# x loaded and turned by columns, projected before it is normalised, and the stick-breaking mask added in PSUM by VectorE

## The chip, the cores and the metric

One core of one Trainium2 chip. The metric is the device time of one execution in microseconds (us); lower is better. The number compared is the median over runs. Clock of TensorE: 2.4 GHz at its upper level, 1.2 GHz at its lower one.

## The reference

One block of a streaming encoder, with a sequence of 512 tokens and width 2048, all in float32:

```python
u = rms_norm(x, norm_gain)                      # x / sqrt(mean(x^2) + eps) * gain, per token
proj = u @ w_in                                 # 2048 -> 13392 columns
# split: q,k,v,z of 8 "sb" heads; q,k,v,z of 8 "sa" heads; q_ix (16 x 64), k_ix (64), w_ix (16); 2 gates
# sb head: z = q.k / sqrt(128), strictly causal (s < t)
#   w[t,s] = exp(log_sigmoid(z) + sum over s<j<t of log_sigmoid(-z[t,j])), 0 where s >= t;  o = w @ v
# indexer: score[t,s] = sum over h of w_ix[t,h] * relu(q_ix[t,h] . k_ix[s]);  top 128 keys of each query
# sa head: softmax over the chosen keys with ALiBi;  o = p @ v
mixed = sigmoid(g_sb) * (o_sb * silu(z_sb)) @ w_branch_sb + sigmoid(g_sa) * (o_sa * silu(z_sa)) @ w_branch_sa
out = rms_norm(x + mixed @ w_out, final_norm_gain)
```

The top-k choice of a query does not change when its scores are all multiplied by one positive number, and relu passes a positive factor through. The gain belongs to a feature, the root-mean-square factor (`rstd` below) to a token.

## The kernel before

**Products.** Each float32 product is made of three TensorE products of rounded parts: a value is copied by ScalarE into a rounded "hi" part, VectorE subtracts to get the "lo" part, and `mm3` adds hi x hi, lo x hi and hi x lo in PSUM. A product has 128 x 128 weights and 512 columns.

**Chunks and strips.** All projections stream their weights. A chunk `c` is 512 output columns (34 chunks in all); it is made of 8 strips `s`, each of two k-tiles of 128 rows (512 KB), loaded by SyncE into one of two buffers `stage`. ScalarE makes `w_hi` (`split_hi`), VectorE `w_lo` (`split_lo`), both two strips ahead (`LEAD`) in a ring of four, and TensorE runs the 24 products of a strip into the four banks `proj`. Each engine has one instruction stream in program order; between the strips other work stands as a list of steps (`chunk(c, steps)`). Semaphores tie the streams: SyncE loads a strip only when `strip_lo` says that the buffer's last user is split.

**The start.** Chunks 0 and 1 make the indexer's queries. `u` must be there transposed (features on partitions): `u_hi`, `u_lo`, 16 k-tiles of 512 tokens. x comes as four row tiles `xs[:, i, :]` of 1 MB. For each, ScalarE sums squares (`sum_of_squares`), VectorE makes `rstd` (`row_scale`, six small steps and a root on ScalarE) and scales the first 512 columns in place (`normal`); TensorE turns them with the identity (`turn_x`), and the copy out of PSUM multiplies by the gain (`turned_u_high`, `turned_u_low`). Only when the fourth row tile is done has tile 0 of `u` all its tokens. Between these transposes TensorE multiplies zeros (`keep_busy`, tile `blank`). The remaining columns are normalised in one go (`normal(i, slice(CW, D_MODEL))`) and turned between the strips of chunk 0, where the 80 columns of the index keys and weights are projected too (`index_keys`, bank `kw_bank`).

**The sb heads.** While chunks 10 to 17 stream, one sb head is worked off beside each. Step 0: scores z into the four banks `attn` (block i holds keys 128i.. against the queries from 128i on). Step 1 to 3: ScalarE takes abs, exp and ln (`e_tile`), VectorE completes softplus(z) and multiplies the 128 x 128 diagonal block by the 0/1 mask `before` (`softplus`). Step 4: TensorE adds to z the negated sums of softplus over later keys (weights `neg_tri`, `neg_one`), and last, with `big_ident` (1e30 times the identity), one 128-column product that puts -1e30 where the key is not before the query. Step 5: ScalarE takes exp.

The order of all of this is written by hand; nothing plans it. The functions that the change touches, with the profile's line numbers:

Of the kernel before, what the change touches and what calls it, by code (L numbers as in the profile page):

```python
# [25 lines left out]
D_MODEL, SEQ = 2048, 512  # L26
# [4 lines left out]
P = 128  # L31
# [30 lines left out]
def build(nc, x, norm_gain, w_in, w_branch_sb, w_branch_sa, w_out, final_gain, out):  # L62
# [57 lines left out]
    blank = at("blank", [CW], R, place["late"] + 4 * P)  # L120

# [24 lines left out]
    big_ident = at("big_ident", [P], R, place["const"] + 4 * P)  # L146
# [31 lines left out]
    def unit(kp, late):  # L178
        return 2 * kp + late

    UNITS = KT
    FIRST_TURNED = {0: 1, 2: 2, 1: 3, 3: 4}
    UNIT_BANK = [attn[j] for j in (0, 1, 3, 2)] + [attn[(j - 4) % 3] for j in range(4, UNITS)]
    BEFORE_IT = {4: 0, 5: 1, 6: 3}
# [7 lines left out]
    x_rows = x[0].rearrange("(i p) d -> i p d", p=P)  # L192
# [10 lines left out]
    x_loaded = [sem(f"x_loaded{i}") for i in range(QT)]  # L203
    gain_loaded, ixw_loaded, consts, masks = sem("gain_loaded"), sem("ixw_loaded"), sem("consts"), sem("masks")
    sumsq, norm_step, rooted, xn_ready = sem("sumsq"), sem("norm_step"), sem("rooted"), sem("xn_ready")
    gain_turned, gain_ready, blank_ready = sem("gain_turned"), sem("gain_ready"), sem("blank_ready")
    xt_done, u_hi_ready, u_lo_ready = sem("xt_done"), sem("u_hi_ready"), sem("u_lo_ready")
    ixw_hi_ready, ixw_lo_ready, kw_done, kw_copied = sem("ixw_hi_ready"), sem("ixw_lo_ready"), sem("kw_done"), sem("kw_copied")
    kix_hi_ready, kix_lo_ready = sem("kix_hi_ready"), sem("kix_lo_ready")
    wix_turned, wix_ready, dist_ready, far_ready = sem("wix_turned"), sem("wix_ready"), sem("dist_ready"), sem("far_ready")  # L210
# [5 lines left out]
    z_done, e_step, e_ready, sp_step, sp_ready = sem("z_done"), sem("e_step"), sem("e_ready"), sem("sp_step"), sem("sp_ready")  # L216
# [46 lines left out]
    with block:  # L263

        @block.sync
        def _(sp):
            for i in range(QT):
                sp.dma_start(xs[:, i, :], x_rows[i]).then_inc(x_loaded[i], 16)
                if i == 0:
                    sp.dma_start(gain_rows[0:KT, :], norm_gain[0].rearrange("(t p) -> t p", p=P)  # L270
                                 ).then_inc(gain_loaded, 16)

            def load_strip(c, s, src):

                if not (isinstance(c, int) and NS * c + s < 2):
                    sp.wait_ge(strip_lo, c * NS + (s - 1))
                sp.dma_start(stage[:, s % 2, :, :], src).then_inc(strip_loaded[s % 2], 16)
                if isinstance(c, int) and NS * c + s == 1:
                    sp.dma_start(ixw[:, :, :], win[:, :, COL_KIX:COL_KIX + KW]).then_inc(ixw_loaded, 16)
# [12 lines left out]
            for c in range(C_QIX, C_SB):  # L292
                load_chunk(c, rows(win), COL_QIX + CW * c)
# [18 lines left out]
        def _(pool):  # L312
# [14 lines left out]
            pool.wait_ge(xn_ready, 2 * QT)  # L327
# [38 lines left out]
        def _(act):  # L366
# [33 lines left out]
            def turned_u_high(n):  # L400

                act.wait_ge(xt_done, FIRST_TURNED[n] if n < 4 else n + 1)
                tokens = slice(2 * P * (n % 2), 2 * P * (n % 2) + 2 * P)
                for j in range(2):
                    k = 2 * (n // 2) + j
                    A(u_hi[:, k, tokens], UNIT_BANK[n][:, 2 * P * j:2 * P * j + 2 * P], ACT.Copy,
                      scale=gain[:, k:k + 1]).then_inc(u_hi_ready, 1)

            def sum_of_squares(i):
                act.wait_ge(x_loaded[i], 16)  # L410
                if i:
                    act.wait_ge(sumsq, i)
                A(junk[:, :], xs[:, i, :], ACT.Square, accum_out=ss[:, i:i + 1]).then_inc(sumsq, 1)

            def root_of(i):
                act.wait_ge(norm_step, 6 * i + 1)
                A(root[:, i:i + 1], var[:, i:i + 1], ACT.Sqrt).then_inc(rooted, 1)

            nc.scalar.preload_act_table_set("sqrt_and_others")
            sum_of_squares(0)  # L420
            root_of(0)
# [974 lines left out]
```

## Time and profile before

| | us |
|---|---|
| median of 3 runs | 1637.13 (1636.83 to 1637.85) |
| the profiled execution | 1636.94 |
| its span, first to last instruction | 1635.3 |
| TensorE busy | 1622.2 (99%) |
| VectorE, ScalarE, GpSimd busy | 768.0 (47%), 588.1 (36%), 16.1 (1%) |
| mean granted TensorE clock | 0.999 |
| moved by DMA | 165.90 MB, 101 GB/s over the span |

Busy time counts an instruction from its start to its end. Matmuls overlap (one of 512 columns takes about 390 ns, the next starts 227 ns after it), so their pace is read from starts, not from the busy time.

### The profile page before, as it was taken

How to read it: one execution, taken by the hardware profiler on the slowest of the kernel's cores; microseconds unless marked ns; L12 is line 12 of the kernel's file. 1: busy time of each engine (PE TensorE's matmuls, PEld its weight loads, DVE VectorE, ACT ScalarE, POOL GpSimd, SP SyncE). 2: the span in 40 equal slices, each digit the busy share in tenths (PEclk: the TensorE clock that was granted, in tenths of full speed). 3: DMA queues.
4: the chain of work that ended last, by engine and by line, in shares of the span. 5: the costliest groups of instructions: out<-in, count | busy, mean ns of one | idle time of the engine just before them, and what ended most of it. 6: DMA issues, size and time to landing. Idle time of an engine off the chain costs nothing.

```text
span 1635.3 us, 20353 instructions
## 1 busy us (share of the span) xinstructions
PE 1622.2 (99%) x7402; PEld 1351.3 (83%) x7402; DVE 768.0 (47%) x1151; ACT 588.1 (36%) x942; POOL 16.1 (1%) x37
## 2 busy tenths in 40 slices
PE   8999999999999999999999999999999999999998
PEld 6888888888888888888888888888888888888886
DVE  5334578622125444455544455445455554444333
ACT  5333333222225454445443233333323533322222
POOL 0000000000000000000000000000000000000000
PEclk9999999999999999999999999999999999999999
DMA  5232323332333323232333232332233422253233
GB/s 203 71 103 78 88 80 90 103 94 86 103 103 91 96 83 88 78 103 83 97 87 115 89 102 84 96 96 85 82 103 95 175 97 96 97 198 125 90 107 116
DMA packets 82043, 165.90 MB, mean 101 GB/s; under 512 B 7104, under 2 KB 7632, under 8 KB 80848
## 3 DMA queue, kind: packets, MB, share of 16 engines
q1 hardware_dynamic: 77808, 150.10, 30.3%
q0 software_dynamic: 3040, 13.63, 2.2%
q10 hardware_dynamic: 1152, 1.57, 0.3%
q8 instruction: 29, 0.48, 0.1%
q14 instruction: 14, 0.11, 0.0%
HBM read 156.90 MB, written 8.39 MB: 101 GB/s over the span
## 4 chain that ended last, share of the span: by engine, by line
PE 99%; DVE 1%; DMA 0%; ACT 0%; issue 0%; SPq 0%; DVEq 0%
PE proj L1130 28%; PE proj L1132 28%; PE proj L1131 28%; PE attn L1131 3%; PE attn L1132 3%; PE attn L1130 3%; PE proj L1198 1%; PE attn L1290 1%; PE attn L1324 1%; PE attn L1252 1%; PE attn L1251 1%; PE attn L1178 0%; PE attn L1295 0%; DMA gain_rows<-in_norm_gain 0%; DVE xs L751 0%; PE attn L1297 0%
## 5 line engine op out<-in xcount | busy, mean ns | idle before, releaser
L1130 PE MATMUL proj<-u_hi,w_hi 128*128 128x512 f32 x1536 | 599.9, 391 | 0.1
L1131 PE MATMUL proj<-u_lo,w_hi 128*128 128x512 f32 x1536 | 598.1, 389 | 0.0
L1132 PE MATMUL proj<-u_hi,w_lo 128*128 128x512 f32 x1536 | 598.0, 389 | 0.0
L696 DVE TENSOR_TENSOR w_lo<-stage,w_hi 128x1024 fp32r<-128x1024 f32 x267 | 325.9, 1223 | 512.5 <-ACT w_hi L374 510.4
L374 ACT ACTIVATE w_hi<-stage 128x1024 fp32r<-128x1024 f32 x267 | 282.2, 1060 | 479.2 <-PE proj L1132 351.4
L1132 PEld LDWEIGHTS proj<-u_hi,w_lo 128*128 128x128 f32 x1536 | 288.4, 188 | 60.2
L1130 PEld LDWEIGHTS proj<-u_hi,w_hi 128*128 128x128 f32 x1536 | 288.5, 188 | 59.5 <-issue 0.5
L1131 PEld LDWEIGHTS proj<-u_lo,w_hi 128*128 128x128 f32 x1536 | 288.5, 188 | 58.7
L390 ACT ACTIVATE area<-proj 128x512 f32 (+1 forms) x80 | 47.8, 597 | 171.4 <-PE proj L1132 171.3
L1130 PE MATMUL proj<-w_hi,u_hi 128*128 128x512 f32 x256 | 99.8, 390 | 0.0
L1131 PE MATMUL proj<-w_lo,u_hi 128*128 128x512 f32 x256 | 99.6, 389 | 0.0
L1132 PE MATMUL proj<-w_hi,u_lo 128*128 128x512 f32 x256 | 99.6, 389 | 0.0
L1130 PE MATMUL proj<-w_hi,area_r 128*128 128x512 f32 x216 | 84.0, 389 | 0.0
L1131 PE MATMUL proj<-w_lo,area_r 128*128 128x512 f32 x216 | 84.0, 389 | 0.0
L1132 PE MATMUL proj<-w_hi,area_r 128*128 128x512 f32 x216 | 84.0, 389 | 0.0
L1132 PEld LDWEIGHTS proj<-w_hi,u_lo 128*128 128x128 f32 x256 | 48.1, 188 | 10.0
L1131 PEld LDWEIGHTS proj<-w_lo,u_hi 128*128 128x128 f32 x256 | 48.1, 188 | 9.9
L1130 PEld LDWEIGHTS proj<-w_hi,u_hi 128*128 128x128 f32 x256 | 48.1, 188 | 9.8
L877 DVE RECIPROCAL og<-og 128x512 f32<-128x512 f32 x16 | 53.7, 3354 | 0.5
L471 ACT ACTIVATE relu<-attn 128x256 f32<-128x256 f32 (+2 forms) x48 | 21.0, 490 | 89.9 <-PE attn L1252 89.9
L818 DVE SCALAR_TENSOR_TENSOR score<-relu,wix,score 128x256 f32<-128x256 f32 (+2 forms) x45 | 27.8, 619 | 47.0 <-ACT relu L471 44.2
L1130 PE MATMUL attn<-u_hi,w_hi 128*128 128x512 f32 x128 | 49.8, 389 | 0.0
(184 smaller groups left out, 1444.9 us busy)
## 6 DMA issues: line engine op xcount, KB each, us to landing
stage<-in_w_in SPq DMA_DIRECT2D x208, 512.0 KB, 3.7
stage<-in_w_out SPq DMA_DIRECT2D x32, 512.0 KB, 3.6
stage<-in_w_branch_sb SPq DMA_DIRECT2D x16, 512.0 KB, 3.6
stage<-in_w_branch_sa SPq DMA_DIRECT2D x16, 512.0 KB, 3.9
xs<-in_x SPq DMA_DIRECT2D x4, 1024.0 KB, 8.1
o_scratch<-og POOLq DMA_DIRECT2D x16, 256.0 KB, 2.3
hres<-in_x POOLq DMA_DIRECT2D x1, 4096.0 KB, 13.6
o_in<-o_scratch POOLq DMA_DIRECT2D x3, 1024.0 KB, 5.9
```

The costliest lines, as they stand in the source:

```text
L374: A(w_hi[:, s % RING, :, :], stage[:, s % 2, :, :], ACT.Copy).then_inc(strip_hi, 1)
L390: A(dst(e), proj[e][:, :], ACT.Copy).then_inc(proj_free, 1)
L471: A(relu[:, n % 2, 0:WQ[qi]], attn[h % 4][:, 0:WQ[qi]], ACT.Relu).then_inc(relu_ready, 1)
L696: V.tensor_tensor(w_lo[:, s % RING, :, :], stage[:, s % 2, :, :], w_hi[:, s % RING, :, :].bitcast(F), ALU.subtract).then_inc(strip_lo, 1)
L818: V.scalar_tensor_tensor(acc, relu[:, n % 2, 0:w], wix[:, qi, h:h + 1], acc, ALU.mult, ALU.add).then_inc(relu_used, 1)
L877: V.reciprocal(og[:, :], og[:, :]).then_inc(silu_step, 1)
L1130: nc.tensor.matmul(out_, a_hi, b_hi, start=start, stop=False, skip_group_check=free)
L1131: nc.tensor.matmul(out_, a_hi, b_lo, start=False, stop=False, skip_group_check=free)
L1132: return nc.tensor.matmul(out_, a_lo, b_hi, start=False, stop=stop, skip_group_check=free)
L1198: nc.tensor.matmul(proj[3][:, :], blank[:, 0:P], blank[:, :], start=True, stop=True)
L1251: nc.tensor.matmul(o_, q, kix_lo[:, 0:WQ[qi]], start=True, stop=False)
L1252: nc.tensor.matmul(o_, q, kix_hi[:, 0:WQ[qi]], start=False, stop=True).then_inc(dots_done, 1)
```

## The change

**x.** SyncE loads x as eight column pairs, `x_loaded[p]`: all 512 tokens of 256 features, 512 KB in runs of 1 KB. They are interleaved with the first strips of weights. The gain's load moves to ScalarE's queue. TensorE turns tile k as soon as its pair is there (four 128 x 128 transposes of raw x), 0 and 1 before the first product, 2 and 3 in the middle of strip 0, the others two strips ahead. Strip 0 runs its four banks for the first k-tile and then for the second, so that it can start with half of its weights split.

**u.** Chunk 0 is projected from x times gain, without the token's factor. Tiles from 4 on, and a second time 0 to 3, are copied to SBUF as "raw" tiles (`turned_raw`), times gain; `u_hi` and `u_lo` are made from these. The sums of squares are taken in halves, beside the strips. `rstd` is brought into a row over the tokens by four more transposes (`rstd_cols`, `rstd_row`), the raw tiles are multiplied by it (`scale_raw`), and `u_hi`, `u_lo` are overwritten with the normalised values from the end of chunk 0 through chunk 1 (`normal_high`, `normal_low`). The index keys are projected after strips 5, 6 and 7 from the raw tiles and scaled by the row; the index weights of the first eight index heads get `rstd` once more, since those heads' queries come from chunk 0.

**The mask.** VectorE makes `hide` (0 where the key is before the query, -1e30 elsewhere) and adds it to the diagonal block of each z in PSUM (`mask_z`) before ScalarE reads z. The multiplication by `before` in `softplus` and the products with `big_ident` are gone; ScalarE's `e_tile` waits for `z_masked` instead of `z_done`.

```diff
-            for i in range(QT):
-                sp.dma_start(xs[:, i, :], x_rows[i]).then_inc(x_loaded[i], 16)
...
+            load_x(0)
+            first_strip(0)
+            load_x(1)
+            first_strip(1)
+            for p in range(2, 5):
+                load_x(p)
+            first_strip(2)
+            for p in range(5, NS):
+                load_x(p)
+            first_strip(3)
+            sp.dma_start(ixw[:, :, :], win[:, :, COL_KIX:COL_KIX + KW]).then_inc(ixw_loaded, 16)
...
@@ ScalarE: the start, and the steps between the strips of chunk 0
+            turned_high(0)
+            act.wait_ge(strip_loaded[0], 16)
+            A(w_hi[:, 0, 0, :], stage[:, 0, 0, :], ACT.Copy).then_inc(first_hi, 1)
+            turned_high(1)
+            A(w_hi[:, 0, 1, :], stage[:, 0, 1, :], ACT.Copy).then_inc(strip_hi, 1)
             split_hi(0, 1)
+            turned_high(2)
+            turned_high(3)
+            for i in range(QT):
+                sum_of_squares(i, 0)
+
+            def in_first(s):
                 def f():
+                    if s + 2 < NS:
+                        turned_pair(s + 2)
+                    if s in (1, 2):
+                        for i in (2 * s - 2, 2 * s - 1):
+                            sum_of_squares(i, 1)
...
+                    elif s == NS - 1:
+                        normal_high(0)
+                        normal_high(1)
...
@@ VectorE: a raw tile, and the steps between the strips of chunk 0
+            def turned_raw(k):
+                dve.wait_ge(xt_done, k + 1)
...
+                V.tensor_scalar(raw_u(k), by_tile(turn_bank(k)[:, :]), gain[:, k:k + 1], None,
+                                ALU.mult).then_inc(raw_ready, 1)
...
+            def in_first(s):
                 def f():
+                    if s + 2 < NS:
+                        for k in (2 * s + 4, 2 * s + 5):
+                            turned_raw(k)
+                        for k in (2 * s + 4, 2 * s + 5):
+                            turned_low(k)
+                    if s == 3:
+                        dve.wait_ge(sumsq, 2 * QT)
...
+                        rsqrt(slice(0, QT), 1, 1)
...
+                            V.tensor_scalar(rstd_cols[:, i, :], neg_one[:, :].bitcast(F), rstd[:, i:i + 1], -1.0,
+                                            ALU.mult, ALU.mult).then_inc(cols_ready, 1)
...
+                    elif s == 4:
+                        dve.wait_ge(cols_turned, 1)
+                        V.tensor_copy(rstd_row[:, :], kw_bank[:, :]).then_inc(row_ready, 1)
...
+                    elif s in (5, 6):
+                        scale_raw(2 * s - 10)
+                        scale_raw(2 * s - 9)
...
@@ VectorE: an sb head
+                def mask_z(o):
+                    t = attn[QT - 1 - o][:, 0:P]
+                    dve.wait_ge(z_done, n * 4 + o + 1)
+                    V.tensor_tensor(t, t, hide[:, :], ALU.add).then_inc(z_masked, 1)
+
...
-                                           ALU.max, ALU.add).then_inc(sp_step, 1)
-                    dve.wait_ge(sp_step, n * 4 + o + 1)
-                    t = full[:, o % 2, 0:P]
-                    V.tensor_tensor(t, t, before[:, :], ALU.mult).then_inc(sp_ready, 1)
+                                           ALU.max, ALU.add).then_inc(sp_ready, 1)
...
                 def s1():
+                    for o in range(QT):
+                        mask_z(o)
                     v_low(n, n + 2 * HEADS)
                     softplus(0)
...
@@ TensorE: the start
-            keep_busy(14)
...
+            keep_busy(1)
+            turn_x(0)
+            turn_x(1)
+            keep_busy(4)
...
@@ TensorE: step 4 of an sb head
-                        nc.tensor.matmul(attn[i][:, 0:P], big_ident[:, :], neg_tri[:, :], start=False, stop=True,
-                                         skip_group_check=True).then_inc(c_done, 1)
+                        m.then_inc(c_done, 1)
```

**How instructions move.** TensorE, from the program's start to the first products of strip 0, before (`blank` is the tile of zeros, `attn` the banks that receive transposes, `proj` those of a chunk):

```order
L1198 MATMUL proj<-blank 128x512 x4
L1204 MATMUL attn<-ident,gain_rows 128x16
L1198 MATMUL proj<-blank 128x512 x14
L1178 MATMUL attn<-ident,xs 128x128 x4
L1198 MATMUL proj<-blank 128x512 x9
L1178 MATMUL attn<-ident,xs 128x128 x4
L1198 MATMUL proj<-blank 128x512 x11
L1178 MATMUL attn<-ident,xs 128x128 x4
L1198 MATMUL proj<-blank 128x512 x8
L1178 MATMUL attn<-ident,xs 128x128 x4
L1198 MATMUL proj<-blank 128x512 x7
L1130 MATMUL proj<-u_hi,w_hi 128x512
```

And the same place of the changed kernel:

```order
L1303 MATMUL proj<-blank 128x512 [waits blank_ready]
L1303 MATMUL proj<-blank 128x512 x3
L1309 MATMUL attn<-ident,gain_rows 128x16 [waits gain_loaded,masks]
L1303 MATMUL proj<-blank 128x512
L1290 MATMUL attn<-ident,xs 128x128 [waits x_loaded0]
L1290 MATMUL attn<-ident,xs 128x128 x7
L1303 MATMUL proj<-blank 128x512 x4
L1241 MATMUL proj<-u_hi,w_hi 128x512 [waits first_lo,u_lo_ready]
```

Ahead of the first product stand eight transposes instead of sixteen and nine products of zeros instead of 53, and the first of them waits for one pair of columns instead of all rows.

ScalarE of the changed kernel, from its first copy of a turned tile to the split of strip 3 (`junk,ssq` is a half sum of squares; before, the sums stood ahead of everything, as four of 2048 elements):

```order
L435 ACTIVATE u_hi<-attn,gain 128x512 [waits xt_done,gain_ready]
L468 ACTIVATE w_hi<-stage 128x512 [waits strip_loaded0]
L435 ACTIVATE u_hi<-attn,gain 128x512 [waits xt_done]
L470 ACTIVATE w_hi<-stage 128x512
L405 ACTIVATE w_hi<-stage 128x1024 [waits strip_loaded1]
L435 ACTIVATE u_hi<-attn,gain 128x512 [waits xt_done] x2
L458 ACTIVATE junk,ssq<-xs 128x1024 [waits x_loaded2,x_loaded3,x_loaded1,x_loaded0]
L458 ACTIVATE junk,ssq<-xs 128x1024 [waits sumsq] x3
L405 ACTIVATE w_hi<-stage 128x1024 [waits strip_loaded0]
L438 ACTIVATE u_hi<-area 128x512 [waits raw_ready] x2
L405 ACTIVATE w_hi<-stage 128x1024 [waits strip_loaded1]
```

The four half sums now stand ahead of the split of strip 2, on which VectorE's part of strip 2 and the load of strip 4 hang.

TensorE, step 4 of an sb head (the two last blocks, `attn2` and `attn3`), before:

```order
L1290 MATMUL attn2<-x_lo_66,neg_tri_98 128x256
L1290 MATMUL attn2<-x_hi_64,neg_tri_98 128x256
L1295 MATMUL attn2<-x_lo_66,neg_one_99 128x128
L1295 MATMUL attn2<-x_hi_64,neg_one_99 128x128
L1297 MATMUL attn2<-neg_tri_98,big_ident_97 128x128
L1290 MATMUL attn3<-x_lo_66,neg_tri_98 128x128
L1290 MATMUL attn3<-x_hi_64,neg_tri_98 128x128
L1297 MATMUL attn3<-neg_tri_98,big_ident_97 128x128
```

And of the changed kernel:

```order
L1414 MATMUL attn2<-x_lo_66,neg_tri_100 128x256
L1414 MATMUL attn2<-x_hi_64,neg_tri_100 128x256
L1419 MATMUL attn2<-x_lo_66,neg_one_101 128x128
L1419 MATMUL attn2<-x_hi_64,neg_one_101 128x128
L1414 MATMUL attn3<-x_lo_66,neg_tri_100 128x128
L1414 MATMUL attn3<-x_hi_64,neg_tri_100 128x128
```

One product of 128 columns is gone from each of the four blocks, and nothing stands in its place.

## Rows read from the trace of the kernel before

**Rows 1.** The page, busy times (part 1) and the last chain (part 4).

```profile
PE 1622.2 (99%) x7402; PEld 1351.3 (83%) x7402; DVE 768.0 (47%) x1151; ACT 588.1 (36%) x942; POOL 16.1 (1%) x37
PE 99%; DVE 1%; DMA 0%; ACT 0%; issue 0%; SPq 0%; DVEq 0%
```

**Rows 2.** Waits of TensorE: us in total, times, longest.

```profile
PE attn L1204 <- DMA gain_rows<-in_norm_gain: 2.6, 1, 2.6
PE proj L1198 <- DVE blank L728: 1.7, 1, 1.7
PE attn L1178 <- DVE xs L751: 0.8, 1, 0.8
```

**Rows 3.** Timeline of TensorE, the start: start us, us.

```profile
6.47 4.82 PE L1198 MATMUL proj<-blank 128*128 128x512 f32 x14
...
21.22 0.47 PE L1130 MATMUL proj<-u_hi,w_hi 128*128 128x512 f32 x1
...
26.56 0.39 PE L1132 MATMUL proj<-u_hi,w_lo 128*128 128x512 f32 x1
27.71 1.09 PE L1178 MATMUL attn<-ident,xs 128*128 128x128 f32 x8 [0.76 <-DVE xs L751]
```

**Rows 4.** Timeline of TensorE: between two strips, and where chunk 2 starts.

```profile
34.13 1.04 PE L1178 MATMUL attn<-ident,xs 128*128 128x128 f32 x8
34.93 0.47 PE L1130 MATMUL attn<-u_hi,ixw_hi 128*80 128x512 f32 x1
...
126.35 0.39 PE L1130 MATMUL proj<-u_hi,w_hi 128*128 128x512 f32 x1
```

**Rows 5.** Tiles xs and stage up to 60 us, in that order.

```profile
DMA to landing us min/median/max: 5.0/8.1/11.1
...
DMA to landing us min/median/max: 3.5/3.7/12.6
```

**Rows 6.** Windows: busy time of each engine, clock, DMA share, GB/s.

```profile
8.00:12.00 4.00, 4.00 (x18) 3.27 (x17) 2.08 (x11) 3.07 (x6) 0.00 (x0) 1.00 1.00 422
12.00:15.00 3.00, 3.00 (x16) 2.46 (x15) 1.91 (x10) 2.56 (x6) 0.00 (x0) 1.00 1.01 391
15.00:18.00 3.00, 3.00 (x17) 2.47 (x16) 1.90 (x8) 2.78 (x4) 0.00 (x0) 1.00 1.07 281
```

**Rows 7.** Groups of 0 to 131 us, by shape: busy us, mean ns.

```profile
L696 DVE TENSOR_TENSOR w_lo<-stage,w_hi 128x1024 fp32r<-128x1024 f32 x19 | 23.1, 1220 | 22.7 <-ACT w_hi L374 22.5
L374 ACT ACTIVATE w_hi<-stage 128x1024 fp32r<-128x1024 f32 x19 | 20.0, 1065 | 21.5 <-PE proj L1132 15.8 <-DMA stage<-in_w_in 5.6
L801 DVE TENSOR_TENSOR area_r<-proj,area_r 64x512 fp32r<-64x512 f32 x16 | 11.0, 689 | 12.4 <-ACT area_r L461 12.1
L461 ACT ACTIVATE area_r<-proj 64x512 fp32r<-64x512 f32 x16 | 9.5, 592 | 13.4 <-PE proj L1132 12.9
L413 ACT ACTIVATE junk<-xs 128x2048 f32<-128x2048 f32 x4 | 7.7, 1914 | 4.3 <-DMA xs<-in_x 3.8 <-ACT gain L423 0.5
L751 DVE TENSOR_SCALAR xs<-xs,rstd 128x512 f32<-128x512 f32 x4 | 1.9, 486 | 0.1
```

**Rows 8.** Timeline of TensorE, step 4 of the second sb head.

```profile
571.57 0.22 PE L1297 MATMUL attn<-neg_tri,big_ident 128*128 128x128 f32 x1
571.63 0.39 PE L1290 MATMUL attn<-x_lo,neg_tri 128*128 128x384 f32 x1
...
572.79 0.27 PE L1297 MATMUL attn<-neg_tri,big_ident 128*128 128x128 f32 x1
572.90 0.27 PE L1290 MATMUL attn<-x_lo,neg_tri 128*128 128x128 f32 x1
```

**Rows 9.** Timelines of TensorE and VectorE, the same head.

```profile
570.77 0.39 PE L1290 MATMUL attn<-x_lo,neg_tri 128*128 128x512 f32 x1
...
548.56 0.29 DVE L893 SCALAR_TENSOR_TENSOR full<-attn,eb 128x128 f32<-128x128 f32 x1 [0.85 <-ACT eb L517]
...
559.72 0.69 DVE L903 TENSOR_TENSOR x_lo<-full,x_hi 128x512 fp32r<-128x512 f32 x1 [0.23 <-ACT x_hi L522]
```

More of the change, by code:

```diff
@@ L120, in build @@
     blank = at("blank", [CW], R, place["late"] + 4 * P)
+    rstd_row = at("rstd_row", [SEQ], F, place["late"] + 4 * P + 4 * CW)
+    rstd_cols = at("rstd_cols", [QT, P], F, work + 14 * TILE)
     SUM_W = (WK[2], WK[1])
@@ L174, in build, with turn_bank, bank_user, keys_slot @@
     kw_bank = attn[3]
[L178 to L184, printed above, removed]
+    TURN_BANKS = 3
+    HEAD_START = 4
+    ROW_SLOT = 4
+    KEY_SLOTS = {5: (0, 1, 2), 6: (3, 4, 5), 7: (6, 7)}
+    def turn_bank(k):
+        return attn[k] if k < HEAD_START else attn[(k - HEAD_START) % TURN_BANKS]
+    def bank_user(k):
+        return k - HEAD_START if k < HEAD_START + TURN_BANKS else k - TURN_BANKS
+    def keys_slot(p):
+        return [slot for slot, pairs in KEY_SLOTS.items() if p in pairs][0]
+    def raw_u(k):
+        return by_tile(area[:, 24 + k, :]) if k < KT // 2 else xs[:, :, P * k - D_MODEL // 2:P * k - D_MODEL // 2 + P]
+    def by_tile(ap):
+        return ap.rearrange("p (i t) -> p i t", i=QT)
     o_dram = nc.dram_tensor("o_scratch", (2 * HEADS, P, SEQ), F, kind="Internal").ap()
@@ new lines, in scale_raw, with normal_low @@
+            def scale_raw(p):
+                for k in (2 * p, 2 * p + 1):
+                    dve.wait_ge(raw_ready, k + 1)
+                    V.tensor_tensor(raw_u(k), raw_u(k), by_tile(rstd_row[:, :]), ALU.mult).then_inc(raw_scaled, 1)
+            def normal_low(p):
+                for k in (2 * p, 2 * p + 1):
+                    dve.wait_ge(un_hi_ready, k + 1)
+                    V.tensor_tensor(by_tile(u_lo[:, k, :]), raw_u(k), by_tile(u_hi[:, k, :].bitcast(F)),
+                                    ALU.subtract).then_inc(un_lo_ready, 1)
@@ new lines, in _, with first_strip @@
+            turn_x(0)
+            turn_x(1)
+            keep_busy(4)
+            def first_strip():
+                for j in range(2):
+                    pe.wait_ge(u_lo_ready, j + 1)
+                    if j == 0:
+                        pe.wait_ge(first_lo, 1)
+                    else:
+                        turn_x(2)
+                        turn_x(3)
+                        pe.wait_ge(strip_lo, 1)
+                    for e in range(4):
+                        cols = slice(P * e, P * e + P)
+                        m = mm3(proj[e][:, :], w_hi[:, 0, j, cols], w_lo[:, 0, j, cols],
+                                u_hi[:, j, :], u_lo[:, j, :], j == 0, False)
+                m.then_inc(strip_used, 1)
@@ L1232, in turn_wix @@
                 m.then_inc(wix_turned, 1)
[L1234 to L1236 removed]
+            chunk(C_QIX + 1, [None] * 6 + [turn_wix], ready=lambda t: pe.wait_ge(un_lo_ready, t + 1))
             def dots(qi, s):
```

300 lines of the change are left out of this document (161 added, 139 removed).

## The prediction

> **What bounds the kernel now.** I read the page first: TensorE is busy 99% of the span, and the chain that ended last is TensorE's own for 99% [rows 1]. So time goes down only where TensorE has fewer products in its stream, or where its useful stream starts earlier. The list of waits then shows how little waiting there is: three waits, 5.1 us together, all of them before 28 us [rows 2]. What the list does not show is that TensorE is "busy" with zeros at the start. In the timeline the first real product of a strip starts at 21.22; before it stand 53 products of zeros and 16 transposes, while x is loaded, summed and scaled [rows 3]. The reader should see that 21.2 us of 1635.3 are a prologue, and that after strip 0 (last product issued at 26.56, its slot over at 26.79) another 0.92 us pass until the transposes at 27.71, which wait for VectorE's scaling of the remaining columns. Behind that TensorE never waits again, so what shortens the prologue should reach the end whole, if the other engines keep up. Chunk 2 starts at 126.35 [rows 4], where both kernels have the same work left; I work out that point for the changed kernel.
>
> **The start, step by step.** A transfer of 512 KB that goes alone lands 3.5 us after its issue; the first 1 MB of x, with others queued behind it, took 5.0 [rows 5]. The difference is 1.5 us for half a megabyte, 350 GB/s. The first pair of columns is such a 512 KB transfer, issued first: at about 0.94, as x is now, so it lands at 4.4. Its runs are 1 KB, which no row shows. The bounds are the 2 KB runs of weights (391 GB/s) and the stretch with the 320-byte rows of the index weights (281 GB/s) [rows 6]; I take 350 for it, nearer to the first, since 1 KB is nearer to 2 KB. Strip 0 is next in the queue, 1.3 us more, and the gain has its own queue and is small, so neither is late: strip 0 by 5.9, gain by 3.6 to 4.5.
> Then a chain: four transposes to 4.8 (0.1 us each, 0.80 for eight [rows 4]; up to twice that at the low clock, so 5.2 with the way to ScalarE), u_hi of tile 0 as ScalarE's 512 elements out of PSUM (592 ns) to 5.8, half of w_hi (half of 1065 ns) to 6.4, half of w_lo (half of 1220 ns, 0.65 with its start) to 7.2, and the way to TensorE [rows 7]. The changed stream has its zeros in the same time: five products and eight transposes. The first product starts at about 7.5 instead of 21.22: 13.7 earlier.
>
> **What TensorE does from there to chunk 2.** Now it takes 126.35 - 21.22 = 105.13 us. Strips and index keys are the same 432 products. Changes:
> - minus 0.92, the wait after strip 0, whose cause (scaling in one go, rows 2) is gone;
> - plus 8 transposes of x that used to stand ahead of 21.22, plus 4 of the factor: 12 x 0.1 = 1.2;
> - the clock. The burst of fourteen products of zeros from 6.47 takes 4.82 us, where at 227 ns each it would need about 3.35 [rows 3]: some 7 or 8 of the fourteen ran at half pace, 0.42 apart, after the wait for the gain (2.6 us, rows 2). The granted clock reads 1.00 in the window from 8 on all the same [rows 6], so I go by the spacing. Ahead of the first product the changed stream has five products of zeros and eight transposes behind the gain, less than that; I let 3 products of strip 0 still be slow, 0.19 each, 0.6 in all. If it were a dozen, 2.3.
> - a wait before strip 2. ScalarE has twelve instructions ahead of its split of strip 2: after the copies of tiles 2 and 3, which end at 12.6, four half sums at half of 1914 ns plus reading the sum, 1.15 each, to 17.2; then w_hi at 1065 ns to 18.3, VectorE's w_lo to 19.5, two raw tiles, then u_lo of tiles 4 and 5. A raw tile is a multiplication by a column out of PSUM. VectorE's 512 elements take 486 ns by tensor_scalar from SBUF and 689 when it reads PSUM in tensor_tensor [rows 7]; these are the bounds, and I take 0.69, the row that reads PSUM. This gives 22.2 for u_lo of tile 5, against 21.5 at which TensorE wants it (7.5 + 11.0 for 48 products + 1.6 + 0.8 of transposes + 0.6): 0.7 late.
> - a wait in front of the four transposes of the factor after strip 4. VectorE has 1.15 + 4 x 0.69 = 3.9 us of work for each strip, against a pace of 5.5 + 0.8 = 6.3. In strip 3's slot it gets some 4.2 more (the factor in seven small steps, four copies of 128 elements, ixw_lo of 1280 elements at the pace of w_lo, 1.5): 8.1, so it falls 1.8 behind, having been 1 to 1.5 ahead: 0.7.
> Together 105.13 - 0.92 + 1.2 + 0.6 + 0.7 + 0.7 = 107.4, so chunk 2 starts at 114.9, 11.45 earlier.
>
> One page bears on the price of the raw tile. The Trainium skill (VectorE: DVE Perf Modes, Why PSUM operands drop a tier) says that a float32 operand in PSUM holds VectorE at its plain rate, the doubled rate of a tensor_scalar being one for SBUF. By that rule 0.69 stands; without it, at 0.49, both waits would shrink to 0.4 together and chunk 2 start 1.0 earlier. No row here shows a tensor_scalar of 512 elements out of PSUM.
>
> The rest of the new work costs nothing as long as its cover lasts. VectorE's fullest slot behind the factor is strip 5's: 1.15 and eight instructions of 0.69 (two raw tiles, two u_lo, four scalings), 6.7 us, against 5.5 + 0.8 + 4.1 (eighteen products of index keys) = 10.4 on TensorE. In chunk 1 it has 1.15 + 4 x 0.69 = 3.9 and ScalarE 1.07 + 2 x 0.6 = 2.3 a strip, under 5.5. The first normalised tiles are written after strip 6 is used; TensorE has then index keys, strip 7 and index keys again, 4.1 + 5.5 + 2.7 = 12.3 us, against 4 x 0.6 + 4 x 0.69 = 5.2 for both pairs. Loads: x and four strips are 6.3 MB, at 350 GB/s 18 us behind 2.0: x's last pair is there about 18, wanted after strip 5, beyond 40. Without that cover each microsecond late would be one of the total.
>
> **The mask.** Behind a 384-column product the product with big_ident takes 0.06 us (571.57 to 571.63), among 128-column ones 0.11 (572.79 to 572.90) [rows 8]. Two of each in a head: 0.34, eight heads: 2.7. For it VectorE gets four additions of 128 elements in PSUM and loses as many multiplications by the 0/1 mask in each head. Reading 128 elements out of PSUM takes softplus's first block 0.29 us [rows 9], which I take for an addition. It stands earlier though: all four wait for z, and v_low and the first softplus are queued behind them, 1.7 us later than now; ScalarE's first e_tile comes 0.3 later and its next split of weights with it. The cover: the last x_lo ends at 560.41 and TensorE asks for it at 570.77, 10.4 us later [rows 9], and weights are split two strips, over 10 us, ahead. Cost 0; a saving of 2.7 on the path, since TensorE has no wait there. The lower bound is 0, if something else fills the slots.
>
> **Sum.** -11.45 - 2.7 = -14.2. The profiled execution took 1636.94 (span 1635.3), which becomes 1622.8; it lies 0.2 under the median of 1637.13, so I predict 1622.9.
>
> **The rivals.**
> - *Forecast*: 1621 to 1625, chance 0.70.
> - *The front goes better*: the raw tile at 0.49, columns at the weights' 391 GB/s, full pace from the first product. Then -13.4 - 2.7: 1621.0, and 1620 if the first pair lands half a microsecond sooner. For it: no row proves any wait. Against: strip 0 must be halved by two engines anyway. 0.08, outside the forecast.
> - *The columns come slowly.* At 200 GB/s, below the worst window, the first product starts at 8.5, and tiles 4 to 9 are late by 0.4 to 1.9 us each, 8 in all; chunk 2 only 4.5 earlier: 1630. Against it: runs of 2 KB do 391. 0.06.
> - *The clock stays low through strip 0.* All 24 products at half pace lose 24 x 0.2 = 4.8 instead of 0.6, but 0.7 of the first late wait is swallowed: 1626.4. For it: the stream has a gap for the gain and one for x, and behind the 2.6 us for the gain the pace was low now too [rows 2, 3]. 0.10.
> - *The mask saves nothing*: 1625.6. Only if TensorE waited there. 0.02.
> - *Slower*: the masks hold up VectorE's queue in each sb head. The place is x_lo and sum_lo before step 4. It costs nothing until the chain through e_tile, softplus and splits is 10.4 us later than now, and eight times the excess from there. To end over 1640.4 it must be 12.6 us late; I find 1.7. 0.02.
> The remaining 0.02 is for two of the small ones together.
>
> **Chances.** A measurement of this kernel tells a change from none at about 0.2%, 3.3 us. Faster by over that (below 1633.9): 0.96; within it 0.02; slower 0.02. The range takes in the forecast, most of the better front and the low clock: 1619.8 to 1627.0.
>
> **What would show it.** The first product of strip 0 in the timeline at 7 to 8 us; waits of TensorE for u_lo before strip 2 and for the factor's copies, both under 1.5 us; none in chunk 1; chunk 2's first product at 114 to 116; raw tiles at 0.69; step 4 of a head 0.34 shorter, with no wait of TensorE for x_lo, sum_lo or z_masked. The prediction is wrong if x's first pair lands after 6, if the waits for u_lo repeat strip by strip, or if products beyond the first ten run 0.42 apart.

## The result, and the profile after

| | before | after |
|---|---|---|
| median, us | 1637.49 (1636.83 to 1637.94, 4 runs) | 1622.35 (1622.05 to 1623.18, 4 runs) |
| the profiled execution | 1636.94 | 1623.18 |
| its span | 1635.3 | 1621.6 |

The ratio is 0.9909, with a 95% interval of 0.9891 to 0.9926: 15.1 us less. The forecast was 1622.9, with a range of 1619.8 to 1627.0. The profiled execution of the changed kernel is the longest of its four; the spans of the other three are 1620.5 to 1620.9. The last section comes back to that 1 us.

The page of the changed kernel, parts 1 and 4, beside [rows 1]:

```profile
PE 1610.9 (99%) x7330; PEld 1340.7 (83%) x7330; DVE 789.1 (49%) x1169; ACT 594.4 (37%) x947; POOL 16.2 (1%) x37
...
PE 97%; ACT 1%; DVE 1%; DMA 0%; issue 0%; SPq 0%; ACTq 0%; DVEq 0%
```

TensorE is still the bound. Its waits, beside [rows 2] (us in total, times, longest):

```profile
PE proj L1303 <- DVE blank L780: 1.7, 1, 1.7
PE proj L1241 <- DVE u_lo L803: 0.5, 1, 0.5
PE attn L1309 <- DMA gain_rows<-in_norm_gain: 0.2, 1, 0.2
PE proj L1241 <- DVE w_lo L820: 0.2, 1, 0.2
```

The wait for the gain fell from 2.6 to 0.2 us and the one for VectorE's scaling is gone. The new ones are two short ones, for `w_lo` and for `u_lo`. TensorE's timeline shows where they stand, beside [rows 3] and [rows 4] (start us, us):

```profile
4.88 1.97 PE L1290 MATMUL attn<-ident,xs 128*128 128x128 f32 x8
6.49 2.06 PE L1303 MATMUL proj<-blank 128*128 128x512 f32 x4
8.71 0.77 PE L1241 MATMUL proj<-u_hi,w_hi 128*128 128x512 f32 x1 [0.16 <-DVE w_lo L820]
9.27 0.63 PE L1242 MATMUL proj<-u_lo,w_hi 128*128 128x512 f32 x1
9.70 0.63 PE L1243 MATMUL proj<-u_hi,w_lo 128*128 128x512 f32 x1
10.13 0.58 PE L1241 MATMUL proj<-u_hi,w_hi 128*128 128x512 f32 x1
10.54 0.39 PE L1242 MATMUL proj<-u_lo,w_hi 128*128 128x512 f32 x1
...
22.37 1.03 PE L1290 MATMUL attn<-ident,xs 128*128 128x128 f32 x8
23.94 0.47 PE L1241 MATMUL proj<-u_hi,w_hi 128*128 128x512 f32 x1 [0.53 <-DVE u_lo L803]
...
42.19 1.04 PE L1290 MATMUL attn<-ident,xs 128*128 128x128 f32 x8
43.30 0.66 PE L1338 MATMUL attn<-ident,rstd_cols 128*128 128x128 f32 x4
...
121.37 0.28 PE L1375 MATMUL attn<-kix_lo,area_r 128*128 128x256 f32 x1
```

The first product starts at 8.71 instead of 21.22. The first four hold 0.41 to 0.56 us each (half pace is about 0.43), those from 10.54 on start 0.23 apart. The slots of the eight transposes at 22.37 are over after 0.79 us, at 23.16, and strip 2 starts at 23.94: 0.78 late. The factor's transposes start 1.11 after those at 42.19: 0.32 late. The last row is the first product of a dot (`dots`), the mark that I use for the two kernels' common ground: before it stood at 131.79, so the front gives 10.4 us. The last residual of the output stands 13.8 us earlier than before. The other 3.4 us come in the eight sb heads, whose spacing is 49.48 us where it was 49.90.

Step 4 of the second sb head, TensorE's timeline, beside [rows 8]:

```profile
560.73 0.34 PE L1414 MATMUL attn<-x_lo,neg_tri 128*128 128x384 f32 x1
560.91 0.35 PE L1414 MATMUL attn<-x_hi,neg_tri 128*128 128x384 f32 x1
...
561.33 0.28 PE L1414 MATMUL attn<-x_lo,neg_tri 128*128 128x256 f32 x1
561.45 0.28 PE L1414 MATMUL attn<-x_hi,neg_tri 128*128 128x256 f32 x1
```

The same places in the kernel before, whose rows after those of [rows 8] are needed here:

```profile
571.86 0.34 PE L1290 MATMUL attn<-x_hi,neg_tri 128*128 128x384 f32 x1
...
572.33 0.33 PE L1290 MATMUL attn<-x_lo,neg_tri 128*128 128x256 f32 x1
572.50 0.28 PE L1290 MATMUL attn<-x_hi,neg_tri 128*128 128x256 f32 x1
```

The whole step took 2.47 us before (570.77 to 573.24) and takes 2.03 now (559.93 to 561.96). Of the 0.44, 0.34 are the four slots that the prediction counted. The other 0.10 stand behind two of them: before, the 384-column product that followed the short one held its slot for 0.23 us (571.63 to 571.86), where it now holds 0.18; the 256-column one 0.17 (572.33 to 572.50) instead of 0.12.

VectorE's and ScalarE's rows at the start, as their timelines give them:

```profile
6.09 0.69 ACT L435 ACTIVATE u_hi<-attn,gain 128x512 fp32r<-128x512 f32 x1 [1.69 <-PE attn L1290]
7.20 0.63 ACT L468 ACTIVATE w_hi<-stage 128x512 fp32r<-128x512 f32 x1 [0.43 <-DMA stage<-in_w_in]
...
18.78 1.04 ACT L405 ACTIVATE w_hi<-stage 128x1024 fp32r<-128x1024 f32 x1
21.78 1.29 ACT L438 ACTIVATE u_hi<-area 128x512 fp32r<-128x512 f32 x2 [1.95 <-DVE area L793]
...
19.86 1.23 DVE L748 TENSOR_TENSOR w_lo<-stage,w_hi 128x1024 fp32r<-128x1024 f32 x1 [3.38 <-ACT w_hi L405]
21.00 1.40 DVE L793 TENSOR_SCALAR area<-attn,gain 128x512 f32<-128x512 f32 x2
22.45 1.35 DVE L803 TENSOR_TENSOR u_lo<-area,u_hi 128x512 fp32r<-128x512 f32 x2
```

The chain before strip 2 reads as follows: behind four half sums ScalarE's split of strip 2 starts at 18.78, VectorE has stood still for 3.38 us and splits from 19.86, makes two raw tiles from 21.00, and u_lo of tiles 4 and 5 ends at 23.80. TensorE could have had it at 23.16. Both sides of this wait move with TensorE's first product: ScalarE's copies of tiles 2 and 3, at 13.03, have waited 2.03 us for the transposes in the middle of strip 0 (12.39), and the sums stand behind them.

### The profile page after: what moved, and what is told of

The parts are those of the page before. It is cut to its first block, busy times and chain, and to the rows that moved or that the text cites. A ratio compares the mean times of both kernels' runs of the same rounds, so it can differ in the third digit from the quotient of the medians.

```text
span 1621.6 us, 20273 instructions
## 1 busy us (share of the span) xinstructions
PE 1610.9 (99%) x7330; PEld 1340.7 (83%) x7330; DVE 789.1 (49%) x1169; ACT 594.4 (37%) x947; POOL 16.2 (1%) x37
## 4 chain that ended last, share of the span: by engine, by line
PE 97%; ACT 1%; DVE 1%; DMA 0%; issue 0%; SPq 0%; ACTq 0%; DVEq 0%
PE proj L1241 28%; PE proj L1242 28%; PE proj L1243 28%; PE attn L1242 3%; PE attn L1243 3%; PE attn L1241 3%; PE attn L1414 1%; PE attn L1447 1%; PE attn L1376 1%; PE attn L1375 1%; ACT junk L458 0%; PE attn L1419 0%; DMA stage<-in_w_in 0%; ACT w_hi L405 0%; DVE w_lo L748 0%
## 5 line engine op out<-in xcount | busy, mean ns | idle before, releaser
L990 DVE TENSOR_TENSOR og<-attn,og 128x512 f32<-128x512 f32 x16 | 11.1, 692 | 81.0 <-PE attn L1243 81.0
```

## The experiments

**One half of the change at a time.** `mask_only` is the kernel before with the mask as VectorE's addition; `front_only` is the changed kernel with the old mask. The core of the first edit (the second is its reverse in the changed kernel):

```diff
+                def mask_z(o):
+                    t = attn[QT - 1 - o][:, 0:P]
+                    dve.wait_ge(z_done, n * 4 + o + 1)
+                    V.tensor_tensor(t, t, hide[:, :], ALU.add).then_inc(z_masked, 1)
...
-                    V.tensor_tensor(t, t, before[:, :], ALU.mult).then_inc(sp_ready, 1)
...
-                        nc.tensor.matmul(attn[i][:, 0:P], big_ident[:, :], neg_tri[:, :], start=False, stop=True,
-                                         skip_group_check=True).then_inc(c_done, 1)
```

> The kernel before with the mask alone moved to VectorE. Theory (two separate parts that add up): each sb head is 0.42 us shorter, as in the changed kernel's trace (heads 49.48 apart instead of 49.90), 3.4 us in all, so 1634.1; step 4 of a head 2.03 us instead of 2.47. By my prediction's term (0.34 a head) it is 1634.8. Rival (TensorE waits for the later softplus somewhere when the start is not also changed): under 2 us, 1635.5 or more.

> The changed kernel with the old mask. Theory (separate parts): chunk 2 starts at 115.9 as in the changed kernel, 10.4 us before the old kernel, heads 49.90 apart; the time is the changed kernel's plus 3.4, 1625.7. Rival (the parts help each other): more than 0.5 us off that sum.

Measured: `mask_only` 1634.28 (1633.63 to 1634.61, 11 runs), `front_only` 1625.94 (1625.77 to 1626.33, 5 runs), the kernel before 1637.65 in the same comparison (15 runs); ratios 0.9979 (0.9970 to 0.9988) and 0.9930 (0.9917 to 0.9944). The mask alone gives 3.4 us, 0.42 a head, the front alone 11.7. Their sum, 15.1, is the whole change: neither part hides or eats the other. What a removed slot is worth is read from the traces, since the interval of `mask_only` (2.0 to 4.9 us) holds the predicted 2.7 as well. The heads of `mask_only` stand 49.48 us apart and its step 4 takes 2.02 us (570.89 to 572.91), as in the changed kernel; the heads of `front_only` stand 49.90 apart. So it is not 0.34 us a head but 0.42 to 0.44.

**Where ScalarE's sums stand.** `sums_split` moves two of the four first half sums behind the split of strip 2 and the tiles 4 and 5.

```diff
-            for i in range(QT):
+            for i in (0, 1):
                 sum_of_squares(i, 0)
...
-                    if s in (1, 2):
+                    if s == 0:
+                        for i in (2, 3):
+                            sum_of_squares(i, 0)
+                    elif s in (1, 2):
```

> The changed kernel with the half sums of squares of row tiles 2 and 3 moved behind the split of strip 2 and the copies of tiles 4 and 5 on ScalarE. Theory (the wait before strip 2 comes from ScalarE's four sums ahead of its split): the split of strip 2 comes 2.4 us earlier, the wait of 0.8 us before strip 2 is gone, no new one before strip 3, chunk 2 starts 0.8 earlier: about 1621.6. Rival (the wait comes from VectorE's raw tiles or from the load of strip 2): the wait stays over 0.5 us, 1622.4.

Measured: 1622.66 (1622.36 to 1622.81, 4 runs), ratio 0.9909 (0.9894 to 0.9924), no gain that can be told from the changed kernel, where 1621.6 was expected. The line that is new in the list of TensorE's waits says why (us in total, times, longest):

```profile
PE attn L1341 <- DVE rstd_cols L851: 0.7, 1, 0.7
```

The wait for `u_lo` before strip 2 is gone, and TensorE now waits 0.7 us for the factor's columns. In its timeline the factor's transposes start at 42.90, 1.73 behind the transposes of x at 41.17, so 0.94 late where it was 0.32. From strip 0's second group of transposes to the first dot it takes 108.85 us, against 108.98 in the changed kernel: 0.13 of the 0.78 was kept. The time had not gone, it had moved. The reason is a loop. In each strip VectorE's raw tiles wait for its `w_lo`, which waits for ScalarE's `w_hi`; and ScalarE's `u_hi` waits for the raw tiles, for 1.95 us in the row at 21.78 above. ScalarE's rows in `sums_split` give the loop's period, with its timeline of strips 3 to 5:

```profile
22.57 1.04 ACT L405 ACTIVATE w_hi<-stage 128x1024 fp32r<-128x1024 f32 x1
25.56 1.29 ACT L438 ACTIVATE u_hi<-area 128x512 fp32r<-128x512 f32 x2 [1.95 <-DVE area L796]
...
28.98 1.04 ACT L405 ACTIVATE w_hi<-stage 128x1024 fp32r<-128x1024 f32 x1
```

From split to split it takes 6.41 us, with two sums in each round behind `u_hi`. TensorE's own strip with its transposes takes 6.33 to 6.37. So nothing was caught up by the time that the factor was due. Without sums in it the same loop took 4.19 us in the changed kernel (18.78 to 22.97), so it is the sums' place in the loop that makes it as long as a strip.

**The sums in ScalarE's pause.** `gap` puts two half sums into exactly that pause, in each of the strips 0 to 3, and none ahead of strip 2's split.

```diff
-            for i in range(QT):
-                sum_of_squares(i, 0)
...
+                    if s < 4:
+                        for i in (2 * (s % 2), 2 * (s % 2) + 1):
+                            sum_of_squares(i, s // 2)
                     if s + 2 < NS:
                         turned_pair(s + 2)
-                    if s in (1, 2):
-                        for i in (2 * s - 2, 2 * s - 1):
-                            sum_of_squares(i, 1)
```

> The changed kernel with all eight half sums of squares in ScalarE's pause between the split of the next strip and the two tiles of u_hi, two for each of the strips 0 to 3, and none ahead of strip 2's split. In the profile of sums_split ScalarE stood still there for 1.95 us a strip, waiting for VectorE's raw tiles, and two sums take 2.3 us. Theory (the 0.8 us before strip 2 and the 0.3 us before the factor's transposes are both the price of where ScalarE's sums stand, and its pause can take them): both waits are gone or under 0.1 us, the stretch from the transposes after strip 0's first half to the first dots is 107.9 instead of 108.98, and the median is 1621.3 (1621.0 to 1621.8), with an allowance for the moment at which the start's pace rises. Rival 1 (the loop ScalarE, VectorE, ScalarE is as long as a strip, so any sum in it delays the tiles of strips 3 to 5): the wait before strip 2 is gone, a wait of 0.5 to 1.0 comes back before strips 4 or 5 or the factor's transposes, 1622.3 to 1622.8. Rival 2 (the sums of the second half now wait for x pairs that land late): a pause over 1 us at strip 2, over 1623.

Measured: 1621.19 (1621.11 to 1621.49, 4 runs), the kernel before 1637.43 (7 runs) beside it, ratio 0.99 (0.9884 to 0.9917). It is the fastest version of this study, level with `gap_half3` below. Waits of TensorE and its timeline:

```profile
PE attn L1307 <- DMA gain_rows<-in_norm_gain: 0.3, 1, 0.3
```

```profile
8.56 0.56 PE L1239 MATMUL proj<-u_hi,w_hi 128*128 128x512 f32 x1
8.96 0.39 PE L1240 MATMUL proj<-u_lo,w_hi 128*128 128x512 f32 x1
...
11.48 1.03 PE L1288 MATMUL attn<-ident,xs 128*128 128x128 f32 x8
...
119.39 0.28 PE L1373 MATMUL attn<-kix_lo,area_r 128*128 128x256 f32 x1
```

The other wait in its list is the 1.7 us for the zeros' tile; the list shows no wait of TensorE from its first product on, and in the timeline the factor's transposes start 0.88 us after those ahead of them, so 0.09 late. From 11.48 to 119.39 it takes 107.91 us, where the changed kernel takes 108.98 (12.39 to 121.37): 1.07 less, nearly all of the two late steps of 0.78 and 0.32. Both were the price of where the sums stood.

**Strip 0 in halves.** `half_strip` loads strip 0 as two transfers of 256 KB, so that its first half can be split before the second is there.

```diff
+                if s == 0:
+                    for j, loaded in ((0, half_loaded), (1, strip_loaded[0])):
+                        sp.dma_start(stage[:, 0, j, :], win[:, j, COL_QIX:COL_QIX + CW]).then_inc(loaded, 16)
+                    return
...
-            act.wait_ge(strip_loaded[0], 16)
+            act.wait_ge(half_loaded, 16)
             A(w_hi[:, 0, 0, :], stage[:, 0, 0, :], ACT.Copy).then_inc(first_hi, 1)
             turned_high(1)
+            act.wait_ge(strip_loaded[0], 16)
```

> The changed kernel with strip 0 loaded as two transfers of 256 KB, one for each k-tile, ScalarE waiting only for the first ahead of its first split. Theory (the first product waits for strip 0's load, which lands 0.4 us after ScalarE is free): the first split starts at 6.8 instead of 7.2 and the first product at 8.3 instead of 8.7; as products run at half pace until about 10.5 anyway, chunk 2 starts only 0.2 earlier: 1622.2. Rival (start and end move together, the pace rises that much earlier too): 0.4 to 0.5 earlier, 1621.9. Rival (two small transfers take longer than one): no gain, or up to 0.5 later.

Measured: 1622.52 (1622.22 to 1622.70, 4 runs), no difference. Timelines of ScalarE and TensorE:

```profile
6.75 0.62 ACT L472 ACTIVATE w_hi<-stage 128x512 fp32r<-128x512 f32 x1
...
8.47 0.61 PE L1246 MATMUL proj<-u_hi,w_hi 128*128 128x512 f32 x1
```

And ScalarE's row of `sums_split`, where strip 0 comes as one load:

```profile
6.77 0.62 ACT L468 ACTIVATE w_hi<-stage 128x512 fp32r<-128x512 f32 x1
```

Beside the changed kernel's profiled execution the half of `w_hi` starts 0.45 sooner and the first product 0.24 sooner. That this is the edit's work is not shown. In `front_only`, `sums_split`, `no_blanks`, `late_7` and `late_15`, which load strip 0 in one piece as the changed kernel does, ScalarE splits it at 6.63 to 6.87 without a wait too, and the first product starts at 8.35 to 8.59. The wait of 0.43 us for the load belongs to the one execution of the changed kernel that has a trace. Two things end together just ahead of the first product here: the fourth zero starts at 8.00 and holds its slot of 0.43 at half pace until 8.43, and `w_lo` ends at 8.33. `gap_half3` takes one zero out, on top of `gap` and this edit (`keep_busy(3)` for `keep_busy(4)`).

> As gap, with strip 0 loaded as two halves of 256 KB and three products of zeros instead of four before the first product. Theory (with strip 0's first half split by 8.2, TensorE's own zeros at half pace were what held the first product at 8.47 in half_strip; one fewer takes 0.5 us from it): the first product starts at 8.0 to 8.1, and the median is 0.3 under that of gap, 1620.7 to 1621.3. Rival 1 (the pace rises a fixed time after the first products of the start, and an earlier product at half pace is worth only half of what it is earlier): 0.1 to 0.2 under gap, not told apart from it. Rival 2 (w_lo or u_lo is not there at 8.0): the first product waits until 8.3 or later, no difference from gap.

Measured: 1621.20 (1621.00 to 1621.33, 4 runs), ratio 0.9899 (0.9883 to 0.9916), the same as `gap`; its second rival came true. Timelines of VectorE and TensorE:

```profile
7.63 0.68 DVE L823 TENSOR_TENSOR w_lo<-stage,w_hi 128x512 fp32r<-128x512 f32 x1
...
8.46 0.77 PE L1244 MATMUL proj<-u_hi,w_hi 128*128 128x512 f32 x1 [0.27 <-DVE w_lo L823]
```

With the zero gone TensorE waits 0.27 us for `w_lo`, which ends at 8.31, behind `u_lo` on VectorE. In every trace with four zeros or fewer the first product starts 0.14 to 0.15 us after `w_lo` ends, and without any zeros (`no_blanks`, below) it starts no sooner, at 8.49. So VectorE's two instructions set the moment, and the zeros only happened to end with them.

**Zeros before the first product.** The pace of the start was a term of the sum and a rival. `no_blanks` takes the four zeros away (no `keep_busy` after the turns of tiles 0 and 1), `more_blanks` makes them fourteen (`keep_busy(14)`).

> The changed kernel without the four products of zeros between the first transposes and the first product. Theory (TensorE's pace rises after it has been kept busy, and these products help): the first product starts at the same 8.7 or 0.1 sooner, but the half pace lasts longer than until 10.5; with some 8 to 12 slow products more, at 0.19 each, 1.5 to 2.3 us slower: 1624. Rival (the pace rises at a fixed moment after launch, or the transposes suffice): the same 4 slow products, 1622.4 or 0.1 less.

> The changed kernel with fourteen products of zeros there instead of four. They end at about 6.5 + 14 x 0.42 = 12.4 if all are slow, or about 11.3 if the pace rises at 10.5 or sooner. Theory (the pace rises with what TensorE was kept busy with, zeros or not): the first product starts at 11.0 to 11.4, all of strip 0 at full pace; against the changed kernel 2.5 later at the start and 0.9 won back, but part of the waits behind (0.8 before strip 2, 0.3 before the factor's transposes) is swallowed: 0.5 to 1.6 slower, 1623.4. Rival (the other engines' queue sets the pace up to strip 2 anyway): no change within 0.5.

Measured: 1624.16 (1623.42 to 1624.98, 5 runs) and 1624.68 (1624.40 to 1625.19, 5 runs), 1.8 and 2.3 slower than the changed kernel. TensorE's timeline in `no_blanks`, and then in `more_blanks`:

```profile
8.49 0.76 PE L1241 MATMUL proj<-u_hi,w_hi 128*128 128x512 f32 x1 [1.56 <-DVE w_lo L820]
...
10.76 0.63 PE L1243 MATMUL proj<-u_hi,w_lo 128*128 128x512 f32 x1
11.19 0.46 PE L1241 MATMUL proj<-u_hi,w_hi 128*128 128x512 f32 x1
```

```profile
6.44 4.56 PE L1303 MATMUL proj<-blank 128*128 128x512 f32 x14
10.84 0.39 PE L1241 MATMUL proj<-u_hi,w_hi 128*128 128x512 f32 x1
```

Without zeros TensorE stands still for 1.56 us, and six products run at half pace, the last of them from 10.76. The traces with four zeros have one to four such products. The 1.8 us are not to be read off the two traces of `no_blanks` and the changed kernel, though: the one is the shortest execution of its five, the other the longest of its four, and their first dots stand only 0.26 us apart (121.63 and 121.37). `late_7` below has the start of the changed kernel, and its first dot stands at 120.47, 1.16 sooner than in `no_blanks`.

With fourteen the first product already has the full pace, but starts at 10.84, 2.1 later than now. None of the waits behind was swallowed by that, although a part had been expected to be. From strip 0's second transposes to the first dot it takes 109.01 us, against 108.98, for the chain to `u_lo` hangs on those transposes. Four zeros fill the time in which nothing else could be done, and a slow product that does work beats a slow zero.

**The slower rival: how late may VectorE be?** `late_7` and `late_15` put 8 and 18 reciprocals of 128 columns (about 0.98 us each from start to start, into a tile that nobody reads any more) ahead of the masks in each sb head.

```diff
+                    for a in range(8):
+                        dve.wait_ge(delayed, n * 8 + a + 1)
+                        V.reciprocal(before[:, :], neg_one[:, :].bitcast(F)).then_inc(delayed, 1)
                     for o in range(QT):
                         mask_z(o)
```

> The changed kernel with eight extra reciprocals of 128 columns on VectorE ahead of the masks in each sb head, some 0.85 us each with their waits, 7 us in all. My slower rival said that the masks' place costs nothing until the chain behind them is 10.4 us later. By it nothing changes: 1622.4 within 1. Rival (the split weights or ScalarE's queue behind the masks have less cover than the softplus chain): TensorE waits for w_lo or sum_lo in each head, 1 us or more a head, 1630 or more.

> The same with eighteen extra reciprocals, some 15 us. By the cover of 10.4 us, 5 us a head must show, 40 us in all: 1662 (the wait of TensorE for x_lo or sum_lo before step 4, or for w_lo before that). If the queue also delays the splits and these delay the loads, more: up to 80. If nothing shows, the cover is larger than I read it.

Measured: `late_7` 1622.23 (1622.14 to 1622.42, 4 runs), no change, though the eight take 7.86 us. VectorE's timeline of the second head:

```profile
485.85 7.86 DVE L1035 RECIPROCAL before<-neg_one 128x128 f32<-128x128 f32 x8
...
553.64 0.69 DVE L1011 TENSOR_TENSOR x_lo<-full,x_hi 128x512 fp32r<-128x512 f32 x1 [0.23 <-ACT x_hi L574]
```

The last `x_lo` of that head ends at 554.33, and TensorE asks for it at 559.02: of 10.7 us of cover in the changed kernel (549.24 and 559.93) 4.7 are left.

`late_15` takes 1672.22 (1670.32 to 1673.02, 5 runs), ratio 1.0210 (1.0196 to 1.0224), 50 us more than the changed kernel, where 40 were expected; its eighteen take 17.7 us a head. Waits of TensorE, its timeline, and two windows of 20 us with one without a wait between them (busy us of PE, PEld, DVE, ACT and POOL, granted clock, DMA share, GB/s):

```profile
PE proj L1245 <- DVE w_lo L748: 31.4, 8, 4.1
```

```profile
509.17 0.79 PE L1245 MATMUL proj<-u_hi,w_hi 128*128 128x512 f32 x1 [4.09 <-DVE w_lo L748]
```

```profile
495.00:515.00 20.00, 15.91 (x64) 12.73 (x63) 17.43 (x28) 9.54 (x21) 0.00 (x0) 0.91 0.14 38
...
535.00:555.00 20.00, 20.00 (x93) 16.74 (x92) 16.15 (x18) 4.69 (x7) 0.00 (x0) 1.00 0.19 52
555.00:575.00 20.00, 16.12 (x64) 13.06 (x63) 17.28 (x27) 12.27 (x24) 0.00 (x0) 0.83 0.24 70
```

TensorE waits once in each head, for 3.9 us, and never for `x_lo`: what VectorE's queue holds back is the weight split behind the masks. And each wait has a tail, since the clock is granted low behind it (0.91 and 0.83 in the two windows, products 0.43 apart). The waits are 31.4 of the 50 us. Behind them some 75 products of 512 columns hold their slots for 0.33 us or more, which makes about 15 of the other 18.

## Why the prediction was right

**The bound and the path.** "What shortens the prologue should reach the end whole": it did. The 10.4 us of the front and the 3.4 of the heads make the 13.8 between the two profiled executions, and the two halves built alone give 11.7 and 3.4 of 15.1. That the forecast lies within 0.6 us of the median is in part luck. Between the two profiled executions the front gave 1.0 less than the 11.45 predicted and the mask 0.7 more than the 2.7, and the changed kernel's profiled execution lies 0.8 above its own median.

**First product at 7.5: it came at 8.71, the term that was most off.** Three parts, from the rows. The first pair landed 3.9 us after its issue at 0.94, so at 4.8, not 4.4. From the first transpose at 4.88 it took 1.21 us to ScalarE's `u_hi` at 6.09, where the prediction had 0.8. Four transposes at half pace (eight take 1.61, 4.88 to 6.49) are 0.8 of that and were allowed for; the 0.4 behind them, until ScalarE starts, were not. Then strip 0 was not there until 7.20, where 5.9 was expected. In the 2.4 us since the pair some 0.8 MB were moved (342 GB/s from 4.80 to 7.20), more than the strip's 0.5, so the loads behind it took part of the rate. This cost 0.43 us of ScalarE's wait in this execution; five of the other traces with the same loads show no such wait, and in them the first product starts at 8.35 to 8.59, still 0.8 to 1.1 later than predicted.

**From there to chunk 2: 107.4 predicted.** The first dots stand 5.4 us behind chunk 2's start, as they did before (131.79 and 126.35), so chunk 2 starts at 115.9, 107.2 after the first product. The parts: the wait after strip 0 is gone, as said. The low clock, 0.6 in the sum, took 0.9 in this execution (8.71, 9.27, 9.70, 10.13, 10.54, each against 0.23). The wait before strip 2, 0.7, was 0.78. The one before the factor's transposes, 0.7, was 0.32. So the stretch came out by two errors that cancel, 0.3 more for the clock and 0.4 less for this wait. The wait before strip 2 is right although both its sides are 1.6 later than predicted (`u_lo` ends at 23.80, not 22.2, and is wanted at 23.16, not 21.5), for the reason given above. `gap` confirms both, since with them gone the same stretch takes 1.07 less.

**The raw tile, 0.69.** The group of the changed kernel (busy us, mean ns):

```profile
L793 DVE TENSOR_SCALAR area<-attn,gain 128x512 f32<-128x512 f32 x8 | 5.6, 743 | 0.0
```

0.74, 8% above the chosen value and a little outside its bounds (two in a row take 1.40, so from start to start it is 0.66); [rows 7] had 486 ns for the same operation from SBUF. The Trainium skill (VectorE: DVE Perf Modes, Why PSUM operands drop a tier) says that a float32 operand in PSUM keeps VectorE at its plain rate, and the trace agrees with it.

**The mask, 2.7.** Right in kind and too small by 0.7. Step 4 is 0.44 shorter, not 0.34: the prediction counted the slots of the four short products and not what the longer product behind each of two of them lost, 0.05 apiece. `mask_only` measures 3.4 by itself. The cost was put at 0, with 10.4 us of cover, and `late_7` bears it out: 7.9 us more in VectorE's queue cost nothing.

**The rivals.** Slow columns: no. From 4 to 18 us the changed kernel moves 351 to 379 GB/s, x in runs of 1 KB and the weights in runs of 2 KB mixed, against 350 assumed; x alone is not seen. Low clock through strip 0: no, four products and not twenty-four, and six even without zeros ahead (`no_blanks`). Mask that saves nothing: no. The slower rival was named with the wrong victim: its place was "x_lo and sum_lo before step 4" with 12.6 us to lose, but `late_15` shows that the weight splits are late first. Such a delay costs more than "eight times the excess", since the low clock adds about half as much again (15 us to 31.4). The better front's chance of 0.08 did not come, though `gap` shows that 1621 was to be had, not by faster tiles but by another order on ScalarE.

## What to carry to other kernels

Work that "lies beside" the bound engine can still be late once; put it where its own engine already waits, and look for that pause in the timeline, as ScalarE's 1.95 us between a split and the tiles. Moving it merely later (`sums_split`) moved the wait to the next reader in line, because with the sums in it the loop of the two helping engines was as long as the bound engine's strip. Price a removed slot by the distance between the starts around it, to the second instruction behind, and not by its own alone.

## What the runs showed of the hardware

The granted clock reads 1.00 in the window from 7 to 10 us of the changed kernel, although products stand 0.43 apart there; only the spacing shows the pace:

```profile
7.00:10.00 3.00, 2.84 (x7) 1.79 (x6) 2.78 (x5) 1.79 (x4) 0.00 (x0) 1.00 1.06 379
```

The moment at which the pace rises differs with the same or nearly the same instructions at the start: 10.5 in the changed kernel's profiled execution, 9.0 in `gap` and 8.9 to 9.1 in `front_only` and `late_7`. Each of the stretches from strip 0's second transposes to the first dot is nonetheless 108.98 to 109.02 us for the changed kernel, `front_only`, `half_strip`, `no_blanks`, `late_7` and `late_15`. So what differs lies ahead of it. The profiled execution of `late_7` took 1622.26 us, 0.92 less than the changed kernel's, and its first dot stands 0.90 sooner: 0.36 because the first product starts sooner (8.35 against 8.71), 0.54 because fewer products are slow. The two together would account for what lies between 1622.05 and 1623.18 us for the changed kernel; its other three executions have no trace, so for them this is inferred from their spans. The Trainium skill (TensorE: Matmul & The Clock Gate, What's actually happening) says that the number of slow products at a start differs from run to run of one kernel. These runs agree: the changed kernel's trace has four, and `late_7`, whose instructions up to there are the same, has one of 0.56 us and one of 0.28. What sets it was not tried.

Why a 128-column product makes the longer one behind it hold its slot 0.05 us longer stays open too; no run here measured it by itself.
